# Which partitions of a slot block hold an expert's rows: the first ones, or every eighth rank beside the next

## What is computed

```python
g_idx = top_k(softmax(t @ w_router_g + b_router_g), 1)       # one of 4 groups
e_top, e_idx = top_k(e_logits of that group, 2)              # 2 of its 8 experts
combine = group probability * softmax over the two logits
out = sum over experts e of (silu(t @ w1[e]) * (t @ w3[e]) * combine[:, e]) @ w2[e]
```

```
41 43 | 35 27 | 28 19 | 34 25 | 35 41 | 44 35 | 24 43 | 30 48
47 26 | 28 23 | 34 33 | 17 32 | 35 22 | 38 29 | 23 39 | 22 24
```

## Time and profile before

| what | us |
| --- | --- |
| median of 3 runs | 659.46 |
| lowest and highest of them | 654.67, 661.25 |
| the profiled execution, its own time | 655.55 |
| its span, first to last instruction | 653.8 |

### The profile page before, as it was taken

How to read it: one execution, slowest core, us unless ns; L and a number is a source line. 1 busy time by engine, 2 the same in 40 slices (tenths; PEclk the granted TensorE clock), 3 DMA queues, 4 the chain that set the end, 5 groups by cost and what they waited for, 6 DMA issues and landing times.

```text
span 653.8 us, 7874 instructions
## 1 busy us (share of the span) xinstructions
PE 599.4 (92%) x3008; PEld 358.0 (55%) x3008; DVE 303.9 (46%) x607; ACT 168.6 (26%) x368; POOL 97.0 (15%) x136
## 2 busy tenths in 40 slices
PE   2699799999999999999999989999999988899785
PEld 0444486877676667754788745444445433344333
DVE  0228986446666564238424474322323222236167
ACT  3025022244334434242103202222223121112010
POOL 2022241079200000000001021211111111100000
PEclk9799899999999999999999999999999999899899
DMA  8994844321763306060755754899999999999963
GB/s 313 398 355 185 336 163 161 129 69 60 266 249 127 132 18 240 15 243 2 309 219 212 292 228 186 341 418 420 419 421 420 418 421 418 420 420 422 385 259 129
DMA packets 41498, 173.85 MB, mean 266 GB/s; under 512 B 6268, under 2 KB 6332, under 8 KB 28660
## 3 DMA queue, kind: packets, MB, share of 16 engines
q1 hardware_dynamic: 34128, 159.40, 61.5%
q0 software_dynamic: 5744, 12.84, 5.4%
q10 hardware_dynamic: 1588, 1.10, 0.5%
HBM read 165.36 MB, written 15.74 MB: 277 GB/s over the span
## 4 chain that ended last, share of the span: by engine, by line
PE 65%; DMA 17%; issue 6%; DVE 6%; POOL 3%; SPq 2%; ACTq 1%; ACT 1%; DVEq 0%; POOLq 0%
DMA arena<-in_w_dram 13%; PE bank L922 11%; PE bank L645 6%; PE bank L647 6%; PE bank L646 6%; PE bank L954 5%; PE bank L735 4%; POOL ss L1887 3%; DMA qkg<-in_k_norm_dram 2%; PE bank L827 2%; PE bank L937 2%; PE bank L829 2%; PE bank L828 2%; PE bank L767 2%; PE bank L669 2%
## 5 line engine op out<-in xcount | busy, mean ns | idle before, releaser
L922 PE MATMUL bank<-arena,hT 128*64 128x512 f32 x352 | 86.9, 635 | 9.2 <-DMA arena<-in_w_dram 7.9
L645 PE MATMUL bank<-hT_high,w_in_parts 128*128 128x512 f32 x160 | 66.3, 414 | 0.0
L647 PE MATMUL bank<-hT_high,w_in_parts 128*128 128x512 f32 x160 | 62.7, 392 | 0.0
L646 PE MATMUL bank<-hT_low,w_in_parts 128*128 128x512 f32 x160 | 62.4, 390 | 0.0
L922 PEld LDWEIGHTS bank<-arena,hT 128*64 128x64 f32 x352 | 24.7, 144 | 51.3 <-issue 41.8
L1206 ACT COPY probs<-bank 128x512 f32<-128x512 f32 x32 | 18.8, 587 | 120.3 <-PE bank L922 120.3
L1616 DVE TENSOR_SCALAR hT<-bank,ab 128x128 f32<-128x128 f32 x64 | 21.9, 405 | 45.4 <-PE bank L907 45.4
L954 PE MATMUL bank<-arena,g1b 128*64 128x512 f32 x176 | 39.7, 593 | 2.6 <-DVE g1b L1631 2.6
L937 PEld LDWEIGHTS bank<-fold,probs 128*128 128x128 f32 x256 | 32.6, 196 | 16.0 <-issue 11.4
L922 PE MATMUL bank<-late,hT 128*64 128x512 f32 x160 | 36.5, 598 | 3.9 <-DMA late<-in_w_dram 3.9
L1643 DVE TENSOR_TENSOR acc<-bank,g2b 128x512 f32<-128x512 f32 x18 | 11.6, 686 | 60.2 <-PE bank L954 60.2
(11 more groups left out here) (286 smaller groups left out, 999.5 us busy)
## 6 DMA issues: line engine op xcount, KB each, us to landing
arena<-in_w_dram SPq DMA_DIRECT2D x66, 1024.0 KB, 22.9
late<-in_w_dram SPq DMA_DIRECT2D x30, 1024.0 KB, 24.2
late<-in_w_ada_dram SPq DMA_DIRECT2D x6, 2048.0 KB, 12.8
arena<-in_w_ada_dram SPq DMA_DIRECT2D x5, 2048.0 KB, 8.9
arena<-in_w_in_dram SPq DMA_DIRECT2D x4, 2048.0 KB, 11.0
late<-in_w_in_dram SPq DMA_DIRECT2D x4, 2048.0 KB, 16.7
y_scratch<-arena POOLq DMA_DIRECT2D x1, 4096.0 KB, 17.7
late<-in_w_out_dram SPq DMA_DIRECT2D x2, 2048.0 KB, 7.9
```

Of the source, the lines that this page charges most:

```text
L645: mm(bank[:, b, :], wH[:, b, k, :], hH[:, k, :], start=k == 0, stop=False)
L646: mm(bank[:, b, :], wH[:, b, k, :], hL[:, k, :], start=False, stop=False)
L647: last = mm(bank[:, b, :], wL[:, b, k, :], hH[:, k, :], start=False, stop=k == 7)
L922: last = mm(bank[r, 2 + n % 2, :].rearrange("p (w f) -> p w f", w=2), xgT[n // 2 % 2][:, k, SLOTS * (n % 2):SLOTS * (n % 2 + 1)], w13[s][: ...
```

## The change

The numbers in `iota_s` take another order. Position 8a + b (a and b from 0 to 7) now holds 1 + a + 8b instead of 1 + 8a + b. So the token of rank r (from 0) of an expert sits in slot 8 (r mod 8) + r div 8 of the block: ranks 0 to 7 go to the partitions 0, 8, 16, ..., 56, ranks 8 to 15 to 1, 9, 17, ..., 57, and so on. Of each run of 8 partitions the first n/8 are filled (rounded up or down) instead of the first n of all 64. Nothing else differs: the same instructions on the same shapes, apart from the iota, whose access pattern has one more dimension.

```diff
 SLOTS = 64
+SLOT_STEP = 8
...
-            g.iota(iota_s, pattern=[[1, SLOTS]], base=1, **kw).then_inc(iotas_ready, 1)
+
+            g.iota(iota_s.rearrange("p (a b) -> p a b", b=SLOT_STEP), pattern=[[1, SLOTS // SLOT_STEP], [SLOT_STEP, SLOT_STEP]],
+                   base=1, **kw).then_inc(iotas_ready, 1)
```

## The result

The changed kernel takes 664.66 us (median of 17 runs, 661.35 to 667.98) and the kernel before 657.56 (17 runs, 654.38 to 661.25; the 659.46 of the table above is of the first three of these). The ratio is 1.0104, with an interval from 1.0084 to 1.0125: 7 us slower. The profiled execution has a span of 660.6 us, 6.8 more than before.

What follows compares the result with a forecast made beforehand. The prediction took the kernel as bound by when the last weights land, set by the DMA engine with most rows: 38 more rows x 0.156 = 5.9 us, 659.46 + 5.9 = 665.4 us, range 658 to 671.

Steps and rivals of the forecast that it cites:

- The mapping of partitions to engines: In gathers and scatters, each engine serves four partitions of the lower and four of the upper half of each 64.
- the two other mappings: Ways to deal partitions to engines: blocks of 8 neighbours (busiest engine 208 rows before), or partition mod 16 (131 rows).
- two readings: Trace evidence for the mapping: small packets burst after 388.45 in the first gather; last load lands at 626.0.
- The busiest engine's rows: Gathers 4 to 15 and scatters 0 to 13: the busiest engine goes from 153 to 191, 38 rows more.
- the price of a row: Each 4 KB row costs 0.156 us by the rate, 5.9 us for 38; by q0's busy time 0.173, 6.6 us.
- Does it reach the end: Expert 30's load moves from 616.05 to 622.0, tail moves as one; reading back moves 5.9, keeping 2.5 us to spare.
- The sign that the waits for weights would grow: L922's waits for weights grow by some 6 us, as much as expert 30's load lands later.
- The rival with an added half clock: One more TensorE half-clock stretch behind the last load adds 3.0 us, together 8.9: 668.4; chance 0.10.
- The share of the DMA engines: From 608 to 618 near 0.5 instead of 1.02 to 0.77, odd engines being done by about 607.
- Faster, by blocks of eight: If engines served 8 neighbouring partitions, the busiest falls from 208 to 118 rows, 14 us less: 645.4; chance 0.06.
- No effect: Engines take descriptors as they come free, or scatters even out the gathers' surplus: 659.5; chance 0.16.
- Late gathers: Gathered rows come after TensorE wants them in six pairs after 500 us, 1 us each: up to 671.4; chance 0.08.

Runs made afterwards that it cites:

- the even order: Kernel before with iota order changed so rank r goes to engine r mod 8 of its expert's eight: 653.02 us, ratio 0.9927.
- the one-after-the-other order: Kernel before with iota order changed to fill one engine's eight partitions, then the next engine's: 666.48 us, ratio 1.0140.
- the doubled scatters: Two kernels issuing every scatter twice: in the order of before 670.35 us, ratio 1.0203; with ranks spread r mod 8 over engines 662.14 us, ratio 1.0060.
- the mirrored one: The changed kernel with each run of eight slots reversed, so odd engines get the rows: 666.24 us, ratio 1.0137 to before.
- the two that take turns: One kernel: even pairs use the changed order, odd pairs the same moved by four partitions; against before 651.26 us, ratio 0.9903.
- the second trace: Trace of the changed kernel run again unaltered, against before: 666.70 us, ratio 1.0121.

## Why the prediction was right

**The mapping of partitions to engines** was read off two rows, and it held: 4 of the lower and 4 of the upper half of each 64. By the two other mappings the even order would have gained 2 us or lost 2 us; it is 4.8 us faster, and the one-after-the-other order, which they would have left as it was or made 2 us slower, is 9.2 us slower.

One of the two readings was wrong in a detail. The earlier trace rows is not the w2 load issued at 594.3: it is the w3 load of expert 31, issued at 592.09 by L520, whose time to land, 29.2 us, that answer gives. It lands at 621.3, and two loads come behind it, not one. The last load so lands at about 626.3; the text said 626.0, by two errors that cancel, which is luck. What the argument rests on, the end of the weights, stands: the first read-back DMA, next in the queue, lands at 617.3 + 11.4 = 628.7, one load (2.5 us) after that.

**The busiest engine's rows, 153 to 191,** and **the price of a row, 0.156**: the price is met by the doubled scatters (0.155 and 0.145), and by the packets in the traces of before and after: a row of 4 KB takes 0.159 us (median), an empty slot 0.009. The product, 5.9 us, was somewhat small: the stage grew by 7.1 and 7.2 us in the two traces of the change and by 7.2 in the mirrored one, and the ratio says 7 us (5.5 to 8.2). The 6.6 that stood as the other bound is nearer. What makes the last 1.2 us was not tried, and the same holds the other way: the even order gained 4.1 us of the stage for 35 rows, 0.117 a row, and the two that take turns 4.1 for 41. It could be that before one engine alone has 153 rows, and in the change eight have 180 to 191, so that the latest of eight counts and no longer the one. Take from each stage 72 loads at 2.50 us and its rows at 0.156: what is left is 1.2 us before and 1.1 with its scatters doubled, where one engine is well ahead of the next, and 1.9 to 3.5 in the orders where two or more are near the most. This fits, but it is an argument, not shown.

**"Does it reach the end": yes, in one trace of the change as said and in the other by another way.** The text let the load for expert 30 land 5.9 us later and the tail move as one, with 2.5 us to spare for the reading back. In the second trace this is so: from the mark at the w2 issue that load lands 7.2 us later than before (628.41 from 421.34, beside 616.05 from 416.19), and from w3 of expert 31 to the end it is 32.7 us beside 32.5. In the first trace the spare was used up: VectorE waited for the read-back rows. Of the changed kernel's read-back line, who waited for it:

```profile
who waited for it (us, times):
  DVE xs L1670: 1.2, 1
```

Before, expert 30's gate-up waited for weights last and ran at half clock, 6.54 us. In this trace the last wait and its half clock fell two experts earlier (5.35 us at 609.19), and the load for expert 30 landed (596.57 + 27.8 = 624.4) as TensorE came to it, so that TensorE's part of the tail was shorter and caught up with the reading back, which is bound to the busiest engines too. From w3 of expert 31 to the end it is 32.5 us before and 30.2 after. This made 2.3 us less of the profiled execution; the rest of its 6.8 is 7.1 in the stage and 2.0 in a later beginning, for which no part of the change is shown. The sign that the waits for weights would grow by some 6 us is not met: from 480 us on they are 12.2 us in the first trace and 16.7 in the second, beside 11.8 before, since more gate-ups ran slowly behind a wait (four of over 5 us in both traces, beside two before) and TensorE came later to the next weights. The rival with an added half clock named a thing that happens and had its cost wrong. In the first trace one such stretch does come behind the last load:

```profile
643.81 5.16 PE bank L955 x16
```

Before, this down projection took 3.65 us. But VectorE adds stored rows beside it: from its hidden values of expert 31 (L1632, before L1631) to drain_last (L1653, before L1652) it is 5.57 us here, 643.47 to 649.04, and 5.48 before, 636.71 to 642.19. The stretch cost 0.1 us. In the second trace the same down projection takes 3.65.

**The share of the DMA engines.** Foretold near 0.5 between 608 and 618 with the odd engines done at about 607; seen from 614 to 628 in the first trace and from about 618 in the second; until then the share was full. Something held the lightly loaded engines back earlier: from 560 to 600 the share reads 0.99 to 1.01 but the bandwidth is only 381 to 404 GB/s in place of 419 to 422. Taken over 560 to 600 (20 us at 400, 10 at 404, 10 at 381) some 0.95 MB is missing, at 26.25 GB/s for an engine 36 us of engine time, 4.5 us for each of eight: 606.5 as foretold, 2.0 for the later start and 4.5 make 613. The packets show how a full share and a low bandwidth go together. These are the packets of SyncE's queue (number, MB, share) from 590 to 600, before and after:

```profile
q1 hardware_dynamic: 566, 4.11, 98.7%
```

```profile
q1 hardware_dynamic: 496, 3.60, 93.2%
```

The mean size is the same, 7.3 KB, but a packet takes 0.279 us before and 0.301 after. That the engines ahead of the others wait inside such packets for their next piece of work, because SyncE's queue lets them run only so far ahead, fits this and the 4.5 us; no run tests it.

**The rivals.** Faster, by blocks of eight: refuted by the first gather and by the even order. No effect: refuted by every run with an order other than that of before. Late gathers: from 480 us on TensorE waits for none in either trace of the change, and two orders that take turns have gathers as lopsided as the change and are the fastest. The Trainium skill (DMA: Bandwidth & Descriptors, "The descriptor swizzle") has the mapping for direct transfers; here the indirect gathers and scatters follow it too, by the ten rows of the table. The row "Partitions per engine: 8 (convention)" under "Specifications" on that page of the Trainium skill doesn't mean neighbours, at least in these DMAs, where the change lost 7 us.

**The base.** The forecast of 665.4 was set on a median of three runs, 659.46, that was 1.9 us above that of seventeen, and the effect was 1.2 us too small; the two nearly cancel against 664.66. That the forecast lies within 0.7 us is so in part luck.

## What to carry to other kernels

When the DMA engines are saturated, count what the busiest single engine has to move, over the whole stage, not the bytes: an indirect DMA whose filled rows are bunched loads some engines and leaves others idle, and bandwidth near the ceiling until shortly before the end doesn't show it. Find out which partitions one engine serves before spreading anything (the order in which small packets of empty slots and large ones appear in an unloaded gather tells), then spread by that rule; here the same idea with the wrong rule cost 7 us and with the right one gained 5 to 6. It is the sum over many DMAs that must be even; a single one may lean, if the next leans the other way.

## What the runs showed of the hardware

- The indirect gathers and scatters over 128 partitions here give an engine partitions 4k to 4k+3 with 4k+32 to 4k+35, in each half of 64: of the three mappings weighed it alone fits the ten stages. A row of 4 KB costs the busiest engine 0.145 to 0.155 us by the doubled scatters (by the other orders 0.10 to 0.19), an empty slot little (a packet of 0.009 us): with 14 more scatters of 128 slots each, the rows alone account for the time, 85 x 0.156 = 13.3 beside 13.1 measured.
- At a share of 0.50 to 0.53 the engines move 208 to 219 GB/s, half of the 420 at a full share: an engine was no faster here while the others were idle.
- The w3 load of expert 31 takes 28.3 to 31.7 us from issue to landing in all ten traces, while the bandwidth in the change falls to 381 GB/s at a share of 0.99. That an engine some 29 us ahead of the slowest gets nothing more from SyncE's queue, and shows as busy, is read from this and not tested.
